# A decoder step on one core: three reorderings where one weight stage ends and the next begins

## What is computed

```
x += 1/2 * gate1 * SwiGLU(adaLN(x))
x +=       gateM * Mixer(adaLN(x))
x += 1/2 * gate2 * SwiGLU(adaLN(x))
adaLN(x) = RMSNorm(x) * g * (1 + scale) + shift
(shift, scale, gate) x 3 = split(silu(c) @ W_ada + b_ada)
SwiGLU(h) = (silu(h @ w1[:, :D_FF]) * (h @ w1[:, D_FF:])) @ w2
```

## Time and profile before

| | us |
|---|---|
| runs before | 1722.26, 1725.96, 1725.70 |
| median | 1725.7 |
| the profiled execution | 1721.22 |
| its span (first to last instruction) | 1719.5 |

### The profile page before, as it was taken

The page is one execution under the profiler, slowest core; times in us unless marked ns, Lnnn a source line. Parts: engine busy times, 40 slices in busy tenths (PEclk is TensorE's granted clock), DMA queues, the critical chain, the costliest instruction groups (busy, mean ns, idle before and its releaser), DMA issues.

```text
span 1719.5 us, 32145 instructions
## 1 busy us (share of the span) xinstructions
PE 1568.5 (91%) x12152; PEld 1436.4 (84%) x12152; DVE 874.1 (51%) x1281; ACT 703.3 (41%) x876; POOL 211.0 (12%) x328
## 2 busy tenths in 40 slices
PE   4699999899899999889999799899988777899997
PEld 2499998797799998779999699799976556799996
DVE  0444443678554443354444442577637786544442
ACT  1433333342433333243333323566545785443332
POOL 7000000194020000000000000222230350000000
PEclk9899999999999999989999879899979998899998
DMA  9776668552366668766655542234563473355452
GB/s 272 231 233 222 222 221 263 175 167 89 98 209 222 221 219 262 228 196 220 220 174 160 180 139 94 87 103 124 178 236 110 138 240 104 98 171 168 141 162 95
DMA packets 269005, 304.79 MB, mean 177 GB/s; under 512 B 9945, under 2 KB 257857, under 8 KB 268792
## 3 DMA queue, kind: packets, MB, share of 16 engines
q1 hardware_dynamic: 260304, 274.96, 50.3%
q0 software_dynamic: 8624, 28.77, 5.0%
HBM read 300.51 MB, written 11.92 MB: 182 GB/s over the span
## 4 chain that ended last, share of the span: by engine, by line
PE 81%; DVE 7%; ACT 5%; DMA 5%; issue 1%; SPq 0%; POOL 0%; ACTq 0%; DVEq 0%; POOLq 0%
PE ps L1925 13%; PE ps L1929 12%; PE ps L1926 12%; PE ps L1907 7%; PE ps L1908 7%; PE ps L1909 7%; PE ps L1939 4%; DMA ada<-in_ada_w_dram 2%; PE ps L2167 2%; PE ps L2169 2%; PE ps L2168 2%; DMA raw<-in_ffn_w_dram 2%; PE ps L2145 2%; PE ps L2015 1%; ACT wH L787 1%
## 5 line engine op out<-in xcount | busy, mean ns | idle before, releaser
L1225 DVE TENSOR_TENSOR wL<-raw,wH 128x2048 fp32r<-128x2048 f32 (+2 forms) x176 | 365.5, 2077 | 423.0 <-ACT wH L787 422.9
L787 ACT ACTIVATE wH<-raw 128x2048 fp32r<-128x2048 f32 (+2 forms) x176 | 306.4, 1741 | 629.5 <-PE ps L1929 285.9
L1907 PE MATMUL ps<-hH,wL 128*128 128x288 f32 x848 | 261.6, 309 | 15.1 <-DVE hL L1282 12.7
L1925 PE MATMUL ps<-hL,wH 128*128 128x288 f32 x976 | 268.0, 303 | 1.8 <-DVE hL L1828 1.8
L1926 PE MATMUL ps<-hH,wH 128*128 128x288 f32 x976 | 263.8, 296 | 0.0
L1909 PE MATMUL ps<-hH,wH 128*128 128x288 f32 x848 | 256.5, 302 | 0.0
L1908 PE MATMUL ps<-hL,wH 128*128 128x288 f32 x848 | 256.4, 302 | 0.0
L1925 PEld LDWEIGHTS ps<-hL,wH 128*128 128x128 f32 x976 | 184.5, 189 | 15.9 <-issue 13.6
L1925 PE MATMUL ps<-hidL,wH 128*128 128x288 f32 x704 | 194.4, 303 | 1.1 <-ACT wH L787 1.1
L1926 PE MATMUL ps<-hidH,wH 128*128 128x288 f32 x704 | 190.2, 296 | 0.0
L1926 PEld LDWEIGHTS ps<-hH,wH 128*128 128x128 f32 x976 | 184.4, 189 | 0.2
(11 more groups left out here) (407 smaller groups left out, 2243.3 us busy)
## 6 DMA issues: line engine op xcount, KB each, us to landing
raw<-in_ffn_w_dram SPq DMA_DIRECT2D x88, 1024.0 KB, 5.1
ada<-in_ada_w_dram SPq DMA_DIRECT2D x72, 1024.0 KB, 5.2
raw<-in_ffn_w_dram SPq DMA_DIRECT2D x32, 768.0 KB, 5.0
raw<-in_ffn_w_dram SPq DMA_DIRECT2D x32, 640.0 KB, 5.9
craw<-in_cache_cmp_kv_dram SPq DMA_DIRECT2D x64, 256.0 KB, 3.5
raw<-in_nsa_w_in_dram SPq DMA_DIRECT2D x10, 1024.0 KB, 5.3
raw<-in_even_w_in_dram SPq DMA_DIRECT2D x8, 1024.0 KB, 5.4
kvp<-in_cache_sel_kv_dram POOLq DMA_DIRECT2D x64, 128.0 KB, 3.1
```

What stands on the lines that cost most here:

```text
L787: nc.scalar.activation(wH[parity][:, 0:k * UW], raw[parity][:, 0:k * UW], ACT.Copy).then_inc(hi_done, 1)
L1225: nc.vector.tensor_tensor(wL[parity][:, 0:k * UW], raw[parity][:, 0:k * UW], wH[parity][:, 0:k * UW].bitcast(F32), ALU.subtract).then_inc( ...
L1907: nc.tensor.matmul(o, l_, rhsH, start=first, stop=False)
L1925: nc.tensor.matmul(ps[:, banks + t, 0:T], wH[parity][:, c:c + P], L[:, k, :], start=first and k == k0, stop=False)
```

## The change

1. SP: in `ffn`, the first round of the loop is written out ahead of it, and its first weight unit goes ahead of the first conditioning transfer. The loop starts at 1.
2. ACT: in the last quarter of an FFN stage, `take_ada` goes ahead of the split of the next stage's unit.
3. DVE: in the last quarter, `pair_update` goes from u = 3 to u = 2, ahead of the lowering of the next stage's unit and of the last `finish_ada`.
4. PE: in `sum_squares`, the sums go ahead of the conditioning unit's products.

```
--- before.py
+++ after.py
@@ -496,9 +496,13 @@
             def ffn(f):
                 base = FFN_BASE[f]
                 t1, t2 = ADA_IN_W1[f], ADA_IN_W2[f]
+                send(base, 0, w1v[f][:, :, 0:UW], KD)
                 if t1 is not None:
                     send_ada(t1, 0, 0, first_ada[t1] - 1)
-                with sp.Fori(0, HALF_PAIRS) as j:
+                send(base + 1, 1, w1v[f][:, :, DFF:DFF + UW], KD)
+                if t1 is not None:
+                    send_ada(t1, 0, UW, first_ada[t1])
+                with sp.Fori(1, HALF_PAIRS) as j:
                     send(base + 2 * j, 0, w1v[f][:, :, bass.ds(j * UW, UW)], KD)
                     send(base + 2 * j + 1, 1, w1v[f][:, :, bass.ds(j * UW + DFF, UW)], KD)
                     if t1 is not None:
@@ -812,9 +816,11 @@
                     for u in range(4):
                         if u == 3 and f < 3:
                             squares(4 * PAIR_STAGE[f] + q, q)
+                        if last and u < 3 and t2 is not None:
+                            take_ada(t2, first_ada[t2] + 3 * q + u)
                         if not last or u < 2 or f < 3 and u == 2:
                             split(n + u + 2, u % 2, KD if last and u >= 2 else W2CUT[(u + 2) % 4 + 1] - W2CUT[(u + 2) % 4])
-                        if u < 3 and t2 is not None:
+                        if not last and u < 3 and t2 is not None:
                             take_ada(t2, first_ada[t2] + 3 * q + u)
 
                 with act.Fori(0, 3) as q:
@@ -1322,7 +1328,7 @@
                 def pair(q, bank, ln, last=False):
                     n = base + KF + 4 * q
                     for u in range(4):
-                        if u == 3:
+                        if u == (2 if last else 3):
                             pair_update(NORM_OF[f], q, bank, n + 3, ln)
                         if not last or u < 2 or f < 3 and u == 2:
                             lower(n + u + 2, u % 2, KD if last and u >= 2 else W2CUT[(u + 2) % 4 + 1] - W2CUT[(u + 2) % 4])
@@ -1958,11 +1964,10 @@
             def sum_squares(k, left):
 
                 third = ADA_AFTER_NORM[k]
-                if third is not None:
-                    ada_unit(third, 0, first_ada[third], count[third, 0])
                 for q in left:
                     sums(k, q)
                 if third is not None:
+                    ada_unit(third, 0, first_ada[third], count[third, 0])
                     turn_ada(first_ada[third])
 
             def ffn(f):
```

## The result

Four runs of the changed kernel took 1706.64 to 1710.47 us, median **1708.47**; four of the kernel before 1722.26 to 1730.42, median 1725.83. The ratio is 0.990, with a 95% interval of 0.9877 to 0.9923. In a second comparison, with more runs, the same kernel had 1707.11 against 1725.8, ratio 0.9889 (0.9872 to 0.9905). So the change saves 17 to 19 us; the forecast was 1708.6. That forecast and median lie only 0.1 us apart is luck: the medians of the same kernel in the two comparisons lie 1.4 us apart.

What follows compares the result with a forecast made beforehand. PE, busy 91% of 1719.5 us, was taken as the bound, so only its idle stretches could shrink. Terms 5.4 + 0.1 + 0.0 + 8.1 + 3.5 = 17.1 us, against the 1725.7 median, gave 1708.6; range 1702 to 1715.

Steps and rivals of the forecast that it cites:

- What bounds it, and where to look: Whole kernel: PE is busy 91% of the span; products stay, so only PE's waits at five touched stage ends can shrink.
- End of the second FFN stage, 8.1 us: Norm there starts at 726.6 instead of 734.66: weights land early, update at 722.75, lowering last wait by 0.5 us.
- End of the third, 3.5 or 4.3 us: Third FFN stage's end: transfer stays late, squares wait behind ACT's split; gain 3.5 with sums at the slow level, 4.3 fast.
- End of the first, 0.1 us; even mixer, 0.0: First FFN end: 0.6 us won by the update, taken back by the uncovered lowering; even mixer's end: sums meet the same wait.
- The start, 5.4 us: Startup into ffn(0): weights land at 58.8, squares start at 57.32, norm starts at 63.9 instead of 69.3.
- The sum, 17.1: Whole kernel: 5.4 + 0.1 + 0.0 + 8.1 + 3.5 = 17.1 us saved, 1.0%.
- The early transfer slows the one ahead of it: Rival, chance 0.06: last startup transfer lands 3.0 us later, start gains 2.4, 14.1 saved in all, 1711.6 us.
- a sign of trouble: Startup: the prediction is wrong if the last conditioning transfer takes over 6 us.
- Takes some of it: Rival, chance 0.10: PE's clock is low at the stage ends; the three large terms give 13.2 us, 1712.5 in all.
- Stays up: Rival, chance 0.07: conditioning products keep PE's clock up across a norm at three starts, 5.4 us more saved, 1703.2.
- A sign that misled: Fourth FFN stage: the prediction is wrong if it begins less than 12 us earlier; expected 17 us earlier.

## Why the prediction was right, point by point

- *What bounds it, and where to look.* Right. Only the stage ends moved; the time between norms at the two ends forecast at 0.0 and 0.1 stayed within 0.5 us.
- *End of the second FFN stage, 8.1 us.* 7.6 to 8.5 by the table. The order of events was as written: the update at once (721.31, PE's last unit ending at 721.27), the lowering behind it. Only the 0.5 us by which the lowering was to be the last wait is not there: the sums took 1.82 us and ended with it. By which part it came was not said clearly enough: the text put the update's new place and the early weights together, and SP's part alone gives all of it.
- *End of the third, 3.5 or 4.3 us.* 2.8 to 4.9. The slow level under the sums (2.29 us) was right, and so was ACT's split ahead of the squares. The spread comes from where the transfer lands.
- *End of the first, 0.1 us; even mixer, 0.0.* 258.8 before, 258.5 and 258.9 now; 139.2 and 139.5 before, 139.6 now. The lowering that lost its cover took back what the early update won, by the rows.
- *The start, 5.4 us.* The path was right and its base was not. From the squares' start to the norm I had 6.6 us (57.3 to 63.9); it took 6.43. The sums took 5.58, where the text had 4.9 to 9.2. What failed was taking the start-up's pace of one execution as given: "The squares run on ACT from 57.32". They ran from 61.43. So the trace shows 63.9 as 67.9. "PE has work without a break from 58.0 on" failed too: PE stood idle for 2.21 us before the last unit's products, and these ran at the slow level, 1.93 us where both profiles of before have 1.07. Counted from the last startup products, the norm comes 4.7 us sooner (13.4 and 13.6 to 8.7). In all six traces with the change's start or a variant of it the first norm stands at 64.6 to 67.9 us, in the three with the start of before at 69.3 to 71.4. The slow level of that one unit takes 0.86 of the gain: in the two kernels whose start is the change's and whose last unit ran at 1.07, it was 7.85 us (56.73 to 64.58, and 57.23 to 65.08), 5.6 to 5.7 less than before. By the medians, taking PE's part away costs 8.4 us. The traces show 6.1 of that behind the last startup products; another 1.5 is that these ran later in that execution (60.44 against 58.99 in the change's second profile), which isn't the part's doing as far as the traces show.
- *The sum, 17.1.* 17.4 and 18.7 by the two comparisons. The terms of the traces, as the mean of the two of before less that of the two of the change, make 4.8 + 0.1 - 0.3 + 8.1 + 3.9 = 16.6.
- *The rivals.* "The early transfer slows the one ahead of it": the first profile looked like it. The last startup transfer of the change, issued at 52.7 (line 494 by itself, 52.5 to 54 us; the second row is its time to landing):

```profile
L494 SPq DMA_DIRECT2D ada<-in_ada_w_dram x1: 368/368/368, 52.7 to 52.7; - x1
DMA to landing us min/median/max: 6.4/6.4/6.4
```

  That is over the 6 us which the prediction had named as a sign of trouble. But the 3.0 us that the rival asked for are nowhere. With early weights behind it, the last startup transfer took 6.4 here and without PE's part, 5.5 in the change again, 5.3 in SP's part alone, 6.6 with the transfers of the odd stage exchanged, 5.2 with the squares first as well, and 6.5 with ACT's squares first at the third stage. Without them it took 5.2 and 5.0 in the two profiles of before, 6.4 with ACT's and DVE's parts alone, and 5.1 with the weights sent later. So over 6 us also occurs with no neighbour, and 5.2 with one. The means are 6.0 with and 5.4 without: whether the neighbour adds about half a us on average stays open. The Trainium skill says that transfers interleave (DMA: Bandwidth & Descriptors, "Issuing engines are not separate DMA queues"); taken for two transfers in one queue, as the prediction tried it, no run here shows it as a delay of 3 us of the first. What pays is the second, 8.9 us for the weights.
- *The clock.* "Takes some of it" came in small: at the second stage the sums took 1.82 us, between the 1.24 and the 2.29 of the two levels, and at the start the last unit's products lost 0.86. "Stays up" did not come: from 6 to 9 us behind the norm's line 1259 or 1265, at each of the three starts with conditioning, PE started 13 instructions at a granted clock of 0.50 to 0.52, in both profiles of before and in both of the change.
- *A sign that misled.* The text said that it would be wrong if the fourth FFN stage began less than 12 us earlier. It began 10.8 us earlier in the first profile (1483.77 and 1473.02), and 14.1 in the second, of the same kernel. Between the two lies the odd mixer, 4.5 us longer in the first (503.34 and 498.86), where nothing was changed. With the same 3579 instructions PE was busy there for 449.4 and 445.8 us, so 3.6 of the 4.5 us is longer products, not waits. What makes them longer was not tried and stays open. The same 503.4 turned up once more, in the kernel with the transfers exchanged and the startup's squares first; all others had 498.4 to 500.9.

## What to carry to other kernels

In a kernel whose order is written by hand, look at each stage end for a first-of-the-next-stage item that stands behind something it doesn't need: a queue entry that waits for a buffer, a product that waits for a transfer. The worth of each move depends on what else is late: SP's part gives 8.0 us alone and 12.0 beside the others (1719.12 less 1707.11), since at the start it needs PE's. And two parts can buy the same time twice: SP's and the one of ACT and DVE give 8.0 and 6.7 alone, but 10.3 and not 14.7 together, since both shorten the second stage's end. An instruction moved behind a waiting one loses the cover that it had, so count it again in its new place; here that ate the whole 0.6 us at the first stage's end.

## What the runs showed of the hardware that I had not expected

- The start-up, 12 MB of transfers with small products between, differs by up to 3.9 us from one execution to the next in the same instructions: the last startup transfer was issued at 50.1 us in one and at 54.0 in another, and took 5.0 to 6.6 us to land.
- The profile's granted clock does not tell the level of these early products. They went from 1.94 to 1.07 us for a unit at 40 us in one execution and at 48 in another, while the granted clock reads 1.00 in both; in the change without PE's part it reads 1.00 from the start to 75 us, with products of 1.94 throughout. Stretches of before and of the change (span, busy of PE, PEld, DVE, ACT, POOL, granted clock, DMA, GB/s):

```profile
40.00:44.00 4.00, 2.66 (x37) 1.39 (x37) 0.41 (x2) 0.80 (x2) 0.00 (x0) 1.00 1.04 343
40.00:44.00 4.00, 3.32 (x23) 1.48 (x21) 0.44 (x3) 0.80 (x2) 0.00 (x0) 1.00 0.80 263
```

- Two transfers of 1 MB with 512-byte rows (line 540) hold SP's queue for 3.4 to 6.0 us until they are issued, against 0.4 to 0.6 for one with 1 KB rows. The weight transfer behind them waits for that too: in the change they began at 949.60 and it was issued at 953.92.
- After only 2.07 us of idle time on PE (the exchange of the two transfers), two sums took 2.19 us, near the 2.29 of the slow level; after 1.85 us at the first stage's end they took 1.24, the fast one. The length of the idle stretch alone doesn't tell which level the next products get.
